# Sample pairs of the sparse-attention layer: block penalty and maximum in one operation, forced blocks held in the probabilities' columns, exponentials, flips and sums in four stretches

## The reference, cut to what matters

```python
p_cmp = masked_softmax(q . k_cmp - slope * dist)          # over 127 compressed blocks
imp   = sum over the 6 heads of p_cmp
score[b] = imp[4b-1] + imp[4b] + ... + imp[4b+3]          # 33 blocks of 64 tokens
score = inf for blocks 0, cur, cur-1                      # forced
idx   = top_k(score, 16)
p_sel = masked_softmax(q . k - slope * dist)              # over the tokens of the 16 blocks
p_win = masked_softmax(...)                               # over the last 512 tokens
o = g0 * p_cmp @ v_cmp + g1 * p_sel @ v + g2 * p_win @ v_win
```

## Time and profile before

| what | us |
|---|---|
| median of 3 runs | 2690.27 |
| lowest, highest | 2686.73, 2692.47 |
| the profiled execution's own time | 2691.06 |
| its span, first to last instruction | 2689.0 |
| of it the four pairs, 2008.0 to 2192.2 | 184.2 |

### The profile page before, as it was taken

One profiled execution on the slowest core, in us unless ns is written; L12 is line 12 of the kernel. 1 busy time (PEld: TensorE's weight loads), 2 busy tenths in 40 slices (PEclk: granted clock), 3 DMA queues, 4 the chain that ended last, 5 costly groups with the idle time before them and its releaser, 6 DMA issues.

```text
span 2689.0 us, 44667 instructions
## 1 busy us (share of the span) xinstructions
PE 2515.4 (94%) x18826; PEld 2291.8 (85%) x18826; DVE 1057.7 (39%) x1532; ACT 612.7 (23%) x885; POOL 376.9 (14%) x471
## 2 busy tenths in 40 slices
PE   7999998999998999999999998997987778999997
PEld 7999997997778999998999997674554557999997
DVE  5433445323325442444442442003654324443442
ACT  3211223222112211122211211003542212211122
POOL 1000001401221000000000003006666401000001
PEclk9999999998799999999999999896898889999999
DMA  5223212203022223222223222311207533213211
GB/s 173 72 88 100 83 60 83 96 33 104 23 88 94 95 70 117 69 73 94 95 70 114 67 79 57 129 48 55 73 23 230 161 76 110 95 57 100 94 59 53
DMA packets 220770, 232.31 MB, mean 86 GB/s; under 512 B 14649, under 2 KB 207466, under 8 KB 220424
## 3 DMA queue, kind: packets, MB, share of 16 engines
q1 hardware_dynamic: 209088, 199.53, 23.7%
q0 software_dynamic: 10912, 28.48, 3.4%
q10 hardware_dynamic: 624, 2.23, 0.2%
HBM read 220.89 MB, written 13.55 MB: 87 GB/s over the span
## 4 chain that ended last, share of the span: by engine, by line
PE 89%; DVE 5%; POOL 2%; ACT 1%; issue 1%; DMA 1%; POOLq 0%; SPq 0%; DVEq 0%; ACTq 0%
PE ps L361 59%; PE ps L1006 6%; PE ps L992 5%; PE ps L979 2%; PE ps L972 2%; PE ps L1878 2%; PE ps L1108 1%; POOL ring L1748 1%; PE ps L1952 1%; PE ps L1963 1%; PE ps L1981 1%; PE ps L2097 1%; DVE h_lo L575 1%; PE ps L2040 1%; PE ps L557 1%
## 5 line engine op out<-in xcount | busy, mean ns | idle before, releaser
L361 PE MATMUL ps<-h_hi,w_split 128*128 128x272 f32 x5632 | 944.3, 289 | 35.8 <-DVE h_lo L575 25.2
L361 PEld LDWEIGHTS ps<-h_hi,w_split 128*128 128x128 f32 x5632 | 801.1, 189 | 39.2 <-issue 30.1
L361 PE MATMUL ps<-h_lo,w_split 128*128 128x272 f32 x2816 | 586.2, 289 | 0.0
L361 PE MATMUL ps<-g_hi,w_split 128*128 128x272 f32 x2816 | 466.3, 287 | 0.0
L361 PEld LDWEIGHTS ps<-h_lo,w_split 128*128 128x128 f32 x2816 | 445.1, 190 | 0.0
L361 PEld LDWEIGHTS ps<-g_hi,w_split 128*128 128x128 f32 x2816 | 396.4, 188 | 0.0
L430 ACT CAST w_split<-ring 128x2048 fp32r<-128x2048 f32 (+2 forms) x148 | 247.3, 1671 | 365.2 <-PE ps L361 363.9
L437 DVE TENSOR_TENSOR w_split<-ring,w_split 128x2048 fp32r<-128x2048 f32 (+2 forms) x152 | 304.9, 2006 | 47.4 <-ACT w_split L430 46.7
L361 PE MATMUL ps<-g_lo,w_split 128*128 128x272 f32 x1408 | 291.4, 288 | 0.0
L475 DVE TENSOR_TENSOR ns<-ps,ns 128x544 f32<-128x544 f32 x88 | 63.8, 725 | 475.5 <-PE ps L361 474.6
L450 ACT ACTIVATE ns<-ns 128x544 f32<-128x544 f32 x88 | 58.0, 659 | 820.2 <-DVE ns L475 820.2
(11 more groups left out here) (395 smaller groups left out, 2356.2 us busy)
## 6 DMA issues: line engine op xcount, KB each, us to landing
ring<-in_w_ffn_in_dram SPq DMA_DIRECT2D x88, 1024.0 KB, 7.5
ring<-in_w_ffn_out_dram SPq DMA_DIRECT2D x48, 768.0 KB, 4.7
ring<-in_w_in_even_dram SPq DMA_DIRECT2D x13, 1024.0 KB, 5.5
pages_t<-in_cache_nsa_kv_dram SPq DMA_DIRECT2D x80, 128.0 KB, 2.2
pages_t<-in_cache_nsa_kv_dram SPq DMA_DIRECT2D x160, 64.0 KB, 2.6
ring<-in_w_ffn_out_dram SPq DMA_DIRECT2D x16, 512.0 KB, 5.4
ring<-in_w_in_odd_dram SPq DMA_DIRECT2D x8, 768.0 KB, 5.6
pages_t<-in_cache_nsa_kv_dram POOLq DMA_DIRECT2D x48, 128.0 KB, 4.0
```

Of the source, the lines that this page charges most:

```text
L361: mm = pe.matmul(ps[:, b + s, 0:HALF], w, v[:, HALF * s:HALF * s + HALF], start=first and q == 0, stop=last and q == 2)
```

## The change

1. **Forced blocks.** `pcS`, the compressed probabilities, gets 132 columns in place of 128, the probabilities stand in columns 1 to 127, and columns 0 and 128 hold 1e30, written once ahead of the pairs. The sum over the heads then carries 132 columns, goes to bank 7 of PSUM, and DVE sums it by four straight from there: the copy to `imp` and two memsets in each pair are gone. POOL's memset of `imp` is gone too.
2. **Penalty and maximum.** The addition of the block penalty and the maximum over 2048 columns become one `tensor_tensor_reduce`; the maximum of the 32 new columns is taken by an operation of its own ahead of the window's maximum, and the last step joins the two.
3. **Four stretches.** The exponential of `sS` is taken in four pieces (512, 512, 512 and 544 columns) with a sum each (`rs_s`); PE flips each piece as it comes; DVE copies the first two, ACT the other two. The window's probabilities and the compressed ones are flipped before, right behind the compression of the next pair, and copied by DVE. The four sums are added and inverted at the end.
4. **Products.** Compressed and window values come first, then the selected ones, which wait tile by tile group for their copies.

```diff
@@ dve_odd, ahead of the pairs
             C.after(dve.memset(band, 0.0))
+            C.after(dve.memset(pcS, 0.0))
+            C.after(dve.memset(pcS[:, 0:1], 1e30))
+            C.after(dve.memset(pcS[:, NCS + 1:NCS + 2], 1e30))
@@ pe_pair
-            pe.matmul(ps[:, 4, 128:128 + NCS], const("same_query"), pcS[:, 0:NCS], start=True, stop=True).then_inc(imp_done, 1)
+            pe.matmul(ps[:, 7, 0:4 * NBLK], const("same_query"), pcS, start=True, stop=True).then_inc(imp_done, 1)
             if not last:
                 pe_compress_pair(pe, i + 1)
-                pe.wait_ge(pre_ready, i + 3)
-            pe.wait_ge(exps_ready, i * 2 + 2)
-            for t in range(16):
-                pe.transpose(ps[:, t // 4, 128 * (t % 4):128 * (t % 4) + 128], sS[:, 128 * t:128 * t + 128], ident)
+            pe.wait_ge(exps_ready, i * 5 + 1)
             for t in range(4):
                 pe.transpose(ps[:, 4, 128 * t:128 * t + 128], sW[:, 128 * t:128 * t + 128], ident)
-            flip(pe, ps[0:TS, 5, 128:256], sS[:, PAST:PAST + TS])
-            flip(pe, ps[0:TS, 5, 256:384], sW[:, 512:512 + TS])
-            flip(pe, ps[0:NCS, 5, 0:128], pcS[:, 0:NCS]).then_inc(tp_done, 1)
-            pe.wait_ge(pTa_ready, i * 3 + 3)
-            pe.wait_ge(pTv_ready, i * 4 + 4)
+            flip(pe, ps[0:NCS, 5, 0:128], pcS[:, 1:1 + NCS])
+            flip(pe, ps[0:TS, 5, 256:384], sW[:, 512:512 + TS]).then_inc(tp_done, 1)
+            if not last:
+                pe.wait_ge(pre_ready, i + 3)
+            for c in range(4):
+                pe.wait_ge(exps_ready, i * 5 + c + 2)
+                for t in range(4):
+                    mm = pe.transpose(ps[:, c, 128 * t:128 * t + 128], sS[:, 512 * c + 128 * t:512 * c + 128 * t + 128], ident)
+                if c == 3:
+                    mm = flip(pe, ps[0:TS, 7, 128:256], sS[:, PAST:PAST + TS])
+                mm.then_inc(tp_done, 1)
+            pe.wait_ge(pTv_ready, i * 6 + 3)
+            pe_pair_values(pe, i)
@@ act_pair
-            act.wait_ge(tp_done, i + 1)
-            for b in range(3):
+            act.wait_ge(negs_ready, i * 2 + 2)
+            for c in range(4):
+                e = sS[:, 512 * c:512 * c + 512 + (TS if c == 3 else 0)]
+                act.activation(e, e, ACT.Exp, bias=mx[:, 1:2], accum_out=rs_s[:, c:c + 1]).then_inc(exps_ready, 1)
+            for b in range(2, 4):
+                act.wait_ge(tp_done, i * 5 + b + 2)
                 act.copy(pT[:, 4 * b:4 * b + 4].rearrange("p t q -> p (t q)"), ps[:, b, :]).then_inc(pTa_ready, 1)
@@ dve_pair
+            C.after(dve.tensor_reduce(mx_s[:, 1:2], sS[:, PAST:PAST + TS], AX.X, ALU.max))
             dve.wait_ge(sk_ready, i * 5 + 5)
             C.after(dve.tensor_reduce(mx[:, 2:3], sW, AX.X, ALU.max))
@@
-            C.after(dve.tensor_copy(imp[:, 1:1 + NCS], ps[:, 4, 128:128 + NCS]))
-            four = imp.rearrange("p (b r) -> p b r", r=4)
-            C.after(dve.tensor_reduce(score[:, 0:NBLK - 1], four[:, 0:NBLK - 1], AX.X, ALU.add))
+            four = ps[:, 7, 0:4 * NBLK].rearrange("p (b r) -> p b r", r=4)
+            C.after(dve.tensor_reduce(score, four, AX.X, ALU.add))
             C.after(dve.tensor_tensor(score[:, 0:NBLK - 1], score[:, 0:NBLK - 1], four[:, 1:NBLK, 0], ALU.add))
-            C.after(dve.memset(score[:, 0:1], 1e30))
-            C.after(dve.memset(score[:, NBLK - 2:NBLK], 1e30))
@@
-            C.after(dve.tensor_tensor(sb_, sb_, blk_add[:, 0:NBLK - 1].unsqueeze(2).broadcast_to([128, NBLK - 1, 64]), ALU.add))
-            C.after(dve.tensor_reduce(mx[:, 1:2], sS, AX.X, ALU.max))
-            dve.tensor_scalar(mx[:, 1:2], mx[:, 1:2], -1.0, None, ALU.mult).then_inc(negs_ready, 1)
+            dve.sem_inc(waited, 1)
+            C.after(dve.tensor_tensor_reduce(out=sb_, in0=sb_,
+                                             in1=blk_add[:, 0:NBLK - 1].unsqueeze(2).broadcast_to([128, NBLK - 1, 64]),
+                                             scale=1.0, scalar=-3e38, op0=ALU.add, op1=ALU.max, accum_out=mx_s[:, 0:1]))
+            dve.tensor_scalar(mx[:, 1:2], mx_s[:, 0:1], mx_s[:, 1:2], -1.0, ALU.max, ALU.mult).then_inc(negs_ready, 1)
```

More of the change, by code:

```diff
@@ L1565, in trunk @@
         kcT_p, vc_p = A.take(32), A.take(128)
-        imp, score, score2, top8 = A.take(132), A.take(NBLK), A.take(NBLK), A.take(8)
+        score, score2, top8 = A.take(NBLK), A.take(NBLK), A.take(8)
         blk_add = A.take(NBLK)
@@ L1583, in trunk @@
         A2.at = A_TAIL
-        qP, eP, g36, pcS = A2.take(2, 64), A2.take(128), A2.take(NH, 3), A2.take(128)
+        qP, eP, g36, pcS = A2.take(2, 64), A2.take(128), A2.take(NH, 3), A2.take(4 * NBLK)
+        mx_s, rs_s = A2.take(2), A2.take(4)
         o_s = A2.take(128)
@@ L1667, in pool_odd @@
             po.wait_ge(h_ready, NK * 5)
-            for z in (cmp_a[:, :, :], cmp_bd[:, :, :], qB[:, :, :], imp[:, :], cvp[:, :, 0:2]):
+            for z in (cmp_a[:, :, :], cmp_bd[:, :, :], qB[:, :, :], cvp[:, :, 0:2]):
                 mz = po.memset(z, 0.0)
                 mz.then_inc(zeroed, 1)
-            po.wait_ge(zeroed, 8)
+            po.wait_ge(zeroed, 7)
             n = 0
@@ L2091, in pe_pair, with pe_pair_values @@
+            pe.wait_ge(pTv_ready, i * 6 + 3)
+            pe_pair_values(pe, i)
+            pe.wait_ge(os_ready, i + 1)
+            pe.transpose(ps[:, 7, 0:128], o_s[:, :], ident).then_inc(ot_done, 1)
+        def pe_pair_values(pe, i):
+            row = lambda b: slice(64 * b, 64 * b + 64)
             for b in range(2):
                 pe.matmul(ps[row(b), 6, 0:128], pT[0:NCS, 20, row(b)], vcS[0:NCS, b], start=True, stop=True)
[L2093 to L2097, removed]
@@ L2101, in pe_pair @@
                         (pT[0:TS, 22, row(b)], kvtok[0:TS, 4, 640:768])
-                    mm = pe.matmul(ps[row(b), 6, 256:384], lhs, rhs, start=(t == 0), stop=(t == 4))
+                    pe.matmul(ps[row(b), 6, 256:384], lhs, rhs, start=(t == 0), stop=(t == 4))
+            pe.wait_ge(selv_in, SELV_0 + PAGES + i * HALF_PAGES)
+            if i > 0:
+                pe.wait_ge(selv_in_b, SELV_B0 + i * HALF_PAGES)
+            for t in range(17):
+                if t in (0, 4):
[4 more added lines that the diff above has]
+                    pe.wait_ge(pTv_ready, i * 6 + 6)
+                for b in range(2):
+                    lhs, rhs = (pT[:, t, row(b)], pages[:, b, t, 384:512]) if t < 16 else \
+                        (pT[0:TS, 21, row(b)], kvtok[0:TS, 4, 384:512])
+                    mm = pe.matmul(ps[row(b), 6, 128:256], lhs, rhs, start=(t == 0), stop=(t == 16))
             mm.then_inc(pvs_done, 1)
-            pe.wait_ge(os_ready, i + 1)
-            pe.transpose(ps[:, 7, 0:128], o_s[:, :], ident).then_inc(ot_done, 1)
         def act_odd(act):
@@ L2203, in act_pair @@
                     act.wait_ge(negc_ready, i + 1)
-                    act.activation(pcS[:, 0:NCS], pcS[:, 0:NCS], ACT.Exp, bias=mx[:, 0:1],
+                    act.activation(pcS[:, 1:1 + NCS], pcS[:, 1:1 + NCS], ACT.Exp, bias=mx[:, 0:1],
                                    accum_out=rs[:, 0:1]).then_inc(expc_ready, 1)
-            for k, (s, m) in enumerate(((sW, 2), (sS, 1))):
-                act.wait_ge(negs_ready, i * 2 + k + 1)
-                act.activation(s, s, ACT.Exp, bias=mx[:, m:m + 1], accum_out=rs[:, m:m + 1]).then_inc(exps_ready, 1)
-                if k == 0 and not last:
-                    act_pre(act, i + 1)
-            act.wait_ge(tp_done, i + 1)
-            for b in range(3):
+            act.wait_ge(negs_ready, i * 2 + 1)
+            act.activation(sW, sW, ACT.Exp, bias=mx[:, 2:3], accum_out=rs[:, 2:3]).then_inc(exps_ready, 1)
+            if not last:
+                act_pre(act, i + 1)
+            act.wait_ge(negs_ready, i * 2 + 2)
[4 more added lines that the diff above has]
+                act.wait_ge(tp_done, i * 5 + b + 2)
                 act.copy(pT[:, 4 * b:4 * b + 4].rearrange("p t q -> p (t q)"), ps[:, b, :]).then_inc(pTa_ready, 1)
@@ L2232, in dve_odd @@
             C.after(dve.memset(band, 0.0))
+            C.after(dve.memset(pcS, 0.0))
+            C.after(dve.memset(pcS[:, 0:1], 1e30))
+            C.after(dve.memset(pcS[:, NCS + 1:NCS + 2], 1e30))
             C.after(dve.tensor_copy(band[:, :, STRIP:STRIP + 9], cmp_a))
             dve.sem_inc(pair_free, 1)
-            per = 28
+            per = 26
             with dve.Fori(0, NB // 2) as i:
```

24 lines of the change are left out of this document (13 added, 11 removed).

## The result

| | us |
|---|---|
| before, median of 5 runs (lowest, highest) | 2688.21 (2686.42, 2692.47) |
| changed, median of 5 runs (lowest, highest) | 2659.40 (2657.32, 2661.17) |
| ratio, 95% interval | 0.9891 (0.9877 to 0.9906) |
| forecast | 2663.7, range 2656 to 2674 |

What follows compares the result with a forecast made beforehand. Whole-block hand-overs between engines, not a full engine, bound the four pairs. Gains of 31.2 us less 0.45, 3.6 and 0.5 give 26.6: 2691.06 to 2664.4, median 0.8 lower, 2663.7 us; range 2656 to 2674.

Steps and rivals of the forecast that it cites:

- The sum: Four pairs: 5.5 plus 25.65 is 31.2 us gained; less 0.45, 3.6 and 0.5 leaves 26.6.
- Ahead of X: DVE's work before the selected scores' exponential starts: 2.55 us earlier in three pairs, nothing in the first.
- the first rival: Fused penalty and maximum on DVE runs at half pace, 4.4 + 0.15 in place of 2.45; 2668 us; chance 0.12.
- Behind X: From the selected scores' exponential start to the products' end: 11.0 us taken; gain 5.5 first pair, 6.0 each other.
- one low spell somewhere in it: One spell at clock 0.50 between exponential's start and products' end gives 10.5 (in flips) to 11.3 us (in products).
- the best case: Exponential's start to products' end wholly at full clock: 3.9 + 5.7 = 9.6 us.
- X + 12.2: Each pair's products end 12.2 us after the exponential's start, with low clock in flips and products, if transposes don't count.
- The window wait: Third pair's last key flips: PE newly waits 3.6 us for windows, landed 2104.5, wanted 2100.9, POOL free about 2098.8.
- the 7.5 that had been its upper bound: Third pair's wait for windows reaches up to 7.5 us with the slowest landing and POOL 1.7 us late.
- the second pair's windows arrive within a us of their need: Second pair's window transfers, issued by POOL from 2059.51, were to come within a us of PE's need.
- The low clock behind a wait: PE's low clock after the third pair's new wait for windows costs 0 to 1.7 us; 0.5 taken.
- Small terms: Three memsets ahead of the first pair, two at 0.13 and one at 0.2, cost 0.45 us once.

Runs made afterwards that it cites:

- alone: Only DVE's edits (forced blocks, penalty and maximum in one operation) on the kernel before; median 2679.89 us, ratio 0.9963.
- the unfused kernel: The changed kernel with penalty addition and maximum as two operations again, no separate maximum over the new columns; median 2669.30 us, ratio 0.9924 to before.
- the changed kernel's two traces: The changed kernel traced at 2659.40 us, then run and traced again with no edit: median 2664.63 us, ratio 0.9896 to before.
- the filler kernel: The changed kernel plus 48 unread transposes of a constant in the last pair, where PE waits for DVE's maxima; median 2665.23 us, ratio 0.9907 to before.

## Why the prediction was right, and where not

The sum forecast 26.6 us for the pairs; the traces show 25.4. It agrees so well because errors cancelled: more gain behind X than forecast, and more loss in and behind the window waits. That is luck in the sum, though most of its mechanisms were seen.

**Ahead of X: right.** Forecast 2.55 us a pair in three pairs; 2.3, 2.5 and 2.5 in the trace, 2.5 alone. The fused operation took 2.29, the first rival (half pace, 4.4) did not happen. The halving for two fp32 sources in SBUF that the Trainium skill states (Vector Engine (DVE) Microarchitecture Reference, section 7) does not show for this form, nor in the trace of before for L632, as the prediction noted. The first pair gained nothing ahead of X, as said.

**Behind X: right in kind, its size too small.** Forecast 5.5 and three times 6.0, 23.5; measured 6.9, 8.1, 7.3 and 5.9, 28.3. The step "one low spell somewhere in it" failed: three pairs met none and ended at X + 9.62, the 9.6 of the best case. The pieces of the sum were right: exponentials 0.71 apart, products 5.69 us at full clock (2076.05 to 2081.74; forecast 5.7). What was missing was the effect of the edit on the clock itself: with its work drawn together PE keeps the high level, so idling removed pays twice (1.3 us of idling ahead of the flips and 9.6 to the end in the second and third pair; 3.2 and 10.7 to 11.4 in these two of the unfused kernel and in the changed kernel's last). What the prediction priced by the Trainium skill's rule that transposes don't count (TensorE: Matmul & The Clock Gate, Part 4), X + 12.2, did not come in any pair (9.6 to 11.4 in the changed kernel's two traces), and in the filler kernel the clock stood at 1.00 behind transposes alone.

**The window wait: right in kind and place, its size too small.** POOL's chain was read correctly: it ran without pause and was free at 2089.04, which is 9.3 more than that, 2098.3, on the earlier trace's scale (forecast 2098.8). The third pair waited 3.7 us (forecast 3.6), and this agreement is luck. On the same scale PE wanted the windows at 2103.8 (forecast 2100.9) and they were there at 2107.5 (forecast 2104.5): both 3 us late, PE by its wait in the second pair and the low clock behind it, the windows by 1.3 us of POOL's idling ahead of the issue and a landing of 7.1 in place of 5.0. In the second trace of the same kernel, where PE was not so late, the wait was 8.3, beyond the 7.5 that had been its upper bound. And "the second pair's windows arrive within a us of their need" failed: 3.9 us. PE came there some 3 us sooner than assumed, 1.4 from the first pair's larger gain and 1.5 because the low clock at that pair's start was gone (in the kernel before its first key flips took 1.62 us, in the changed one 1.03; in the changed kernel's second trace the spell was there again, and the wait only 2.5); and the two transfers needed 8.3 us from their first issue to the last landing (2049.78 to 2058.1), where 5.8 had been assumed, beside 16 other pages on full engines. The flips of before that this reading rests on:

```profile
2062.77 1.62 PE L2040 MATMUL ps<-cst,pages_t 128*128 128x128 f32 x8
```

**The low clock behind a wait: too small.** 0.5 taken. From the last key flips to the last evacuation a pair needs 3.3 us at full clock; the second took 5.6 and the third 4.6: 3.6 together.

**Small terms.** The memsets cost 0.5 (PE's first wait 1.79 in place of 1.28 us), as said; they lie ahead of the stage. Within it: 28.3 + 7.3 behind and ahead of X, + 1.4 net for low spells at pairs' starts (gone in the second and fourth, new in the third), - 7.6 - 3.6 for the waits and what follows them, - 0.5 for slightly longer hand-overs: 25.3 against 25.4 seen.

**The time itself.** The median lies 4.3 us under the forecast. Two of these come from the median of before, which went from 2690.3 to 2688.2 as runs were added; the rest is 2.2 us more gain than summed, which is within what the clock ahead of the pairs does between executions.

Of the stages' spread of 2 to 3 us between executions of one kernel nearly all is the clock: in the changed kernel's two traces the third windows landed at the same time, and the second trace lost 1.0 us at low clock behind that wait and 1.6 at the fourth pair's start. Left open: why a low spell comes in one execution and not in another, and how the landing times would be with the transfers thinned out.

## What to carry to other kernels

Where a chain of engines hands over whole blocks, first take out of the chain what need not be in it (copies that can run under other products, flips whose data is there early), and only then cut the blocks: here the first gave about 6 us a pair (5.6 to 6.8), the second, added to it, half a us at full clock. When a stage gets shorter, list every transfer whose buffer comes free inside it and put its queue's fixed work beside the new length: what was hidden by 3 us becomes the next wait, and a second buffer, not another queue, is what removes it. A queue with a fixed chain of work sets the pace of everything that waits for its end: edits ahead of such a wait must be judged by their own piece of the trace, since the stage hides them. Compare stages, not totals, where the clock of another stage moves the total by more than the edit.

## What the runs showed of the hardware that was not expected

A `tensor_tensor_reduce` with two fp32 sources in SBUF, one of them broadcast, ran at the addition's pace, 2.29 us for 2048 columns plus 0.08 for reading the maximum. Transposes alone held TensorE at 2.4 GHz (48 of them in the last pair, clock 1.00 behind them in place of 0.72). Two window transfers of 0.5 MB each needed 5.8 us in the first pair and 8 to 12 when POOL's and SP's pages filled the DMA engines. And two executions of the very same program began the pairs 17 us apart (changed kernel, 2000.1 and 2017.1), with a granted clock of 0.94 and 0.90 in the first mixer, while POOL issued the third pair's windows 90.2 us after that beginning in both.
